# Weight sums of a seven-product matmul made in DRAM by accumulating DMAs, with DVE work of three places moved

## The reference, cut to what matters

```
layer 0: x += fox_mixer(rms_norm(x))            # 16 heads of 64, causal softmax with forget gates
         x += square(relu(h @ w_up)) @ w_down   # "ff_a", hidden width 4096
layer 1: x += mla_mixer(rms_norm(x))            # 8 heads, low-rank q and k/v, rotated parts of q and k
         x += square(relu(h @ w_up)) @ w_down   # "ff_b"
         x = rms_norm(x, final_g)
second block, conditioned on c:
         mod = silu(c) @ ada_w + ada_b          # ada_w is 1024 x 6144; six vectors of 1024
         x += g_t * norm(token_mixer(norm(x) * (1 + sc_t) + sh_t))
         x += g_c * norm(conv_ffn(norm(x) * (1 + sc_c) + sh_c))
```

## Time and profile before

| | |
|---|---|
| median of 3 runs | 1982.93 us |
| the profiled execution | 1981.71 us, span 1980.0 us |
| PE busy | 1961.3 us, 99% of the span |
| weight loads of PE | 1640.2 us, 83% |
| DVE busy | 1341.7 us, 68% |
| ACT busy | 894.3 us, 45% |
| POOL busy | 60.4 us, 3% |
| HBM traffic | 205.66 MB read, 2.13 MB written |

### The profile page before, as it was taken

One profiled execution on the slowest core, in us unless ns is written; L12 is line 12 of the kernel. 1 busy time (PEld: TensorE's weight loads), 2 busy tenths in 40 slices (PEclk: granted clock), 3 DMA queues, 4 the chain that ended last, 5 costly groups with the idle time before them and its releaser, 6 DMA issues.

```text
span 1980.0 us, 29280 instructions
## 1 busy us (share of the span) xinstructions
PE 1961.3 (99%) x10404; PEld 1640.2 (83%) x10404; DVE 1341.7 (68%) x2145; ACT 894.3 (45%) x1417; POOL 60.4 (3%) x114
## 2 busy tenths in 40 slices
PE   9999999999999999999999999999999999999999
PEld 7777789898987887898988788778888888888888
DVE  6555579687777776797787769574444686563545
ACT  4555554445444554544444443474333544432333
POOL 0000000000110110000001100000000000000000
PEclk9999999999999999999999999999999999999999
DMA  4332243323562114523226513211322412223232
GB/s 158 86 85 85 75 148 129 106 79 98 184 205 78 52 49 157 179 69 106 96 99 214 190 46 104 74 64 65 96 96 98 151 43 85 96 95 105 88 99 91
DMA packets 61292, 209.05 MB, mean 106 GB/s; under 512 B 7160, under 2 KB 10232, under 8 KB 61200
## 3 DMA queue, kind: packets, MB, share of 16 engines
q1 hardware_dynamic: 49920, 168.32, 25.8%
q0 software_dynamic: 10560, 37.28, 6.0%
q10 hardware_dynamic: 720, 2.23, 0.3%
HBM read 205.66 MB, written 2.13 MB: 105 GB/s over the span
## 4 chain that ended last, share of the span: by engine, by line
PE 94%; DVE 4%; ACT 1%; DMA 1%; issue 1%; SPq 0%; DVEq 0%; ACTq 0%
PE bank L893 23%; PE bank L895 23%; PE bank L894 23%; PE bank L1216 4%; PE bank L1218 4%; PE bank L1217 4%; PE bank L1016 1%; PE bank L1091 1%; PE bank L1075 1%; PE bank L998 1%; PE bank L1001 1%; PE bank L1043 1%; PE bank L949 1%; PE bank L951 1%; PE bank L950 1%
## 5 line engine op out<-in xcount | busy, mean ns | idle before, releaser
L893 PE MATMUL bank<-b_hi,w_hi 128*128 128x512 f32 x2060 | 813.0, 395 | 6.6 <-DVE w_lo L2764 4.0
L895 PE MATMUL bank<-b_hi,w_lo 128*128 128x512 f32 x2060 | 802.9, 390 | 0.0
L894 PE MATMUL bank<-b_lo,w_hi 128*128 128x512 f32 x2060 | 802.7, 390 | 0.0
L893 PEld LDWEIGHTS bank<-b_hi,w_hi 128*128 128x128 f32 x2060 | 387.2, 188 | 95.9 <-issue 8.2
L895 PEld LDWEIGHTS bank<-b_hi,w_lo 128*128 128x128 f32 x2060 | 387.0, 188 | 81.0
L894 PEld LDWEIGHTS bank<-b_lo,w_hi 128*128 128x128 f32 x2060 | 387.4, 188 | 80.2 <-issue 2.4
L2764 DVE TENSOR_TENSOR w_lo<-w_raw,w_hi 128x1024 fp32r<-128x1024 f32 (+3 forms) x259 | 306.8, 1185 | 210.2 <-ACT w_hi L1810 209.5
L1810 ACT ACTIVATE w_hi<-w_raw 128x1024 fp32r<-128x1024 f32 (+3 forms) x259 | 265.5, 1025 | 263.3 <-PE bank L895 253.6
L3916 DVE SCALAR_TENSOR_TENSOR arena<-bank,vec,arena 128x511 f32<-128x511 f32 x88 | 65.7, 749 | 85.8 <-ACT arena L2658 80.5
L1216 PE MATMUL bank<-parts,w_hi 128*128 128x256 f32 x384 | 108.7, 283 | 3.3 <-DVE x L3113 3.3
L1218 PE MATMUL bank<-parts,w_lo 128*128 128x256 f32 x384 | 107.9, 281 | 0.0
(11 more groups left out here) (398 smaller groups left out, 2537.9 us busy)
## 6 DMA issues: line engine op xcount, KB each, us to landing
w_raw<-in_wstream SPq DMA_DIRECT2D x253, 512.0 KB, 3.5
arena<-in_ada POOLq DMA_DIRECT2D x48, 512.0 KB, 4.3
plain<-in_wseven SPq DMA_DIRECT2D x24, 512.0 KB, 5.0
early<-in_wseven SPq DMA_DIRECT2D x24, 512.0 KB, 6.8
w_raw<-in_wstream SPq DMA_DIRECT2D x12, 384.0 KB, 3.0
arena<-crow POOLq DMA_DIRECT2D x16, 256.0 KB, 4.8
w_raw<-in_wstream SPq DMA_DIRECT2D x10, 256.0 KB, 2.6
x<-in_xT ACTq DMA_DIRECT2D x4, 512.0 KB, 6.6
```

Source lines behind the costliest of these rows:

```text
L893: nc.tensor.matmul(dst, whi, rhs_hi(k), start=(k == 0), stop=False)
L894: nc.tensor.matmul(dst, whi, rhs_lo(k), start=False, stop=False)
L895: last = nc.tensor.matmul(dst, wlo, rhs_hi(k), start=False, stop=(k == n - 1))
```

## The change

1. **Sums in DRAM.** A DRAM tensor `seven_sums` takes the sums of all 24 units. POOL makes them in *turns* (`sum_turn`): in turn t it copies two units' four blocks (group t), adds two block columns (group t - 1), one (group t - 2) and one (group t - 3), all DMAs with `accum_op=add` but the copy, each turn behind a wait for all DMAs of the turn before. Turns 0 to 9 stand in the fox attention, one behind each `rows` and then back to back; turns 10 to 14 in the mla attention. SP waits for the sums before a feed-forward's first load. `two`, `three` and `four` go; SP loads each of the seven operands by a DMA of 256 KB into a ring of eight slots.
2. **Rotated low parts** of the second attention are made by DVE (`queries_low`) ahead of the low values.
3. **Conditioning**: of mla_out's six, three stay (tiles 3 to 5), and the wait for the row of silu(c) moves from its start to tile 3; ff_b has one beside every second early up tile and every unit but the first of a chunk (18, in a third place with a single buffer), six in its last up tiles and none behind.
4. **ff_b's last down projection** is written out: each panel's split ahead of the adds, and the splits of three mixer panels one by one between them, not all three ahead.

PE's instructions and their order are the same.

```diff
+        SEVEN_RING = 8
+        GROUP = 2
+        ada_at = [..., ([plain[:, 6:8, :].rearrange("p a t -> p (a t)")] * 2, early[:, 6:8, :].rearrange("p a t -> p (a t)"))]
+        ADA_EARLY, ADA_UP, ADA_POST, ADA_FIRST = 6, 9, 6, 3
+        sum_rows = nc.dram_tensor("seven_sums", (2 * UNITS * P, 4 * T), F32, kind="Internal").ap()
@@ SP
-            def load_seven(n):
-                if n >= 2:
-                    sp.wait_ge(seven_lo, seven_count(SEVEN * (n - 1) - 1))
-                for h in range(2): ...
+            def load_seven(i):
+                if i >= SEVEN_RING and i % GROUP == 0:
+                    sp.wait_ge(seven_lo, seven_count(i - SEVEN_RING + GROUP - 1))
+                n, o = i // SEVEN, i % SEVEN
+                src, at = (seven_rows, PIECE[o]) if PIECE[o] is not None else (sum_rows, SUM_AT[o])
+                sp.dma_start(seven_raw(i), src[n * P:(n + 1) * P, at * T:(at + 1) * T]).then_inc(...)
@@ SP, ahead of the first seven loads of a feed-forward
                         sp.wait_ge(free, count)
+                        sp.wait_ge(sum_in, sum_count(SUM_GROUPS[run] + 3))
@@ POOL
+            def sum_turn(turn):
+                pool.wait_ge(sum_in, sum_count(turn))
+                for back, (to, src, at) in enumerate(((slice(0, 4 * T), seven_rows, slice(0, 4 * T)),
+                                                      (slice(0, 2 * T), seven_rows, slice(T, 3 * T)),
+                                                      (slice(2 * T, 3 * T), sum_rows, slice(0, T)),
+                                                      (slice(3 * T, 4 * T), sum_rows, slice(2 * T, 3 * T)))):
+                    if 0 <= turn - back < SUM_GROUPS["ff_b"]: ...
+                            pool.dma_start(sum_rows[units, to], src[units, at], accum_op=ALU.add).then_inc(sum_in, 16)
             rows(0, 0)
             rows(1, 1)
+            sum_turn(0)
+            for p in range(2, FOX_PAIRS):
+                pool.wait_ge(row_min, 6 * p - 6)
+                rows(p, p % 2)
+                sum_turn(p - 1)
+            for turn in range(FOX_PAIRS - 1, FOX_PAIRS + 1):
+                sum_turn(turn)
             pool.wait_ge(ctx_lo, FOX_PAIRS)
             pool.dma_start(ada_at[1][1], d["cvec"].to_broadcast([P, D])).then_inc(ada_cin, 16)
+            sum_turn(FOX_PAIRS + 1)
             pool.wait_ge(ada_silu, 1)
...
-            with pool.Fori(0, MLA_HEADS // 2) as hh:
-                for m in range(2):
-                    pool.wait_ge(rope_hi, 2 * hh + (m + 3))
-                    pool.tensor_tensor(qr_part[1][m], q_rope[m], qr_part[0][m].bitcast(F32), ALU.subtract).then_inc(rope_lo, 1)
+            for turn in range(FOX_PAIRS + 2, SUM_TURNS):
+                sum_turn(turn)
@@ DVE, mla_step
                     low_context(h - 2, 0, h + (CTX0["mla"] - 1))
+                if project:
+                    queries_low(h, m)
@@ DVE, mla_out
-                    lambda: low_context(MLA_HEADS - 1, 0, CTX0["mla"] + MLA_HEADS), lambda: dve.wait_ge(ada_cin, 48), fresh=4)
+                    lambda: low_context(MLA_HEADS - 1, 0, CTX0["mla"] + MLA_HEADS), nothing, fresh=4)
@@ DVE, end of ff_b
+                last_add(0, 0)
+                for k in range(2, KT):
+                    w_split(last + 1 + k)
+                    last_add(k - 1, (k - 1) % 2)
+                    last_post(k - 2, k % 2)
+                    if k % 2 == 0:
+                        mix_low(k // 2 - 1)
```

More of the change, by code:

```diff
@@ L683, in program, with sum_count @@
         wflat = d["wstream"]
-        def seven_src(n):
-            size = 4 * P * T
-            return d["wseven"][n * size:(n + 1) * size].rearrange("(p c) -> p c", p=P)
+        seven_rows = d["wseven"].rearrange("(r c) -> r c", c=4 * T)
+        sum_rows = nc.dram_tensor("seven_sums", (2 * UNITS * P, 4 * T), F32, kind="Internal").ap()
+        def sum_count(turn):
+            return 16 + 16 * sum(min(max(turn - back, 0), SUM_GROUPS["ff_b"]) for back in range(4))
         block = ctx.enter_context(nc.Block())
@@ L2150, in seven_ffn @@
                 j = first + n - 1
-                def last_square(j):
-                    square(j)
-                    if run == "ff_b":
-                        for p in range(MIX_W):
-                            mix_split(p)
-                segment(run, first + n, KT, last_mid, nothing, lambda: last_square(j), fresh=1)
+                if run == "ff_a":
+                    segment(run, first + n, KT, last_mid, nothing, lambda: square(j), fresh=1)
+                    return last_mid
+                square(j)
+                w_split(first + n + 1)
+                for k in range(2, KT):
+                    w_split(first + n + k)
+                    last_mid(k - 2, k % 2)
+                    if k % 2 == 0:
+                        mix_split(k // 2 - 1)
+                last_mid(KT - 2, 0)
                 return last_mid
@@ L3166, in up_tiles @@
                         else:
[L3167 to L3171 removed]
+                            low(SEVEN * QUAD * seven_chunk(run, c))
+                            low(SEVEN * QUAD * seven_chunk(run, c) + 1)
                         if not last:
@@ L3180, in up_tiles @@
                         up_conditions(run, j)
+                        if run == "ff_b":
+                            tile_condition(c, j - (first if c else 0))
                 w_split(0)
@@ L3208, in seven_ffn @@
                             w_half(c, first, i + 3 - end)
-                        if i % SEVEN == 0:
-                            four(at // SEVEN)
-                        if i % SEVEN == 2 and i + 5 < end:
-                            two(at // SEVEN + 1)
-                        if i % SEVEN == 4 and i + 3 < end:
-                            three(at // SEVEN + 1)
+                        if run == "ff_b":
+                            chunk_condition(c, i)
                         if i == 1:
@@ L3246, in lead1 @@
                         dve.sem_inc(x_sum, 2)
-                        mix_splits()
-                segment(run, last + 1, KT, last_add, last_post, lead0, lead1)
+                if run == "ff_a":
+                    segment(run, last + 1, KT, last_add, last_post, lead0, lead1)
+                    return last_add, last_post
+                w_split(last + 1)
+                lead0()
+                w_split(last + 2)
+                lead1()
+                last_add(0, 0)
+                for k in range(2, KT):
+                    w_split(last + 1 + k)
+                    last_add(k - 1, (k - 1) % 2)
+                    last_post(k - 2, k % 2)
+                    if k % 2 == 0:
+                        mix_low(k // 2 - 1)
                 return last_add, last_post
```

158 lines of the change are left out of this document (82 added, 76 removed).

## The result

The changed kernel takes 2003.4 us (median of 4 runs, 2000.53 to 2010.2) beside 1982.7 us before (4 runs, 1982.1 to 1983.48): ratio 1.0109, 95% interval 1.0083 to 1.0135. It is slower by 1.1%, where 1975.2 us had been forecast. The profiled execution is the fastest of the four: 2000.53 us, span 1998.7, 18.7 us more than before.

The account below looks back on a forecast made before the run. PE, busy 1961.3 of 1980.0 us, was taken as the bound, so only its stalls count. -3.9 - 2.1 - 3.05 + 1.4 = -7.7 gave 1974.0 us profiled, median 1975.2, own range 1973 to 1979.

Parts of the forecast that it names:

- the turn's length: POOL's DRAM sums: a full turn takes 20 us, between 15 and 28, so decay rows, panels and conditioning stay hidden.
- The prediction's 38 us: Estimated full turn if reads and writes both count against 358 GB/s; PE would lose some 85 us; chance 0.02.
- Its rival: Border from attention to ff_a: turns beyond 25.6 us make DVE wait at conditioning; 1997 us at 28; chance 0.13.
- The panels double and no more: Panel loads beside turns: a panel's own 1.3 us of transfer at 409 GB/s doubles at most; about 11 us allowed.
- TensorE's pace doesn't suffer: Whole kernel: DMA traffic alone does not slow PE's matmuls, it can only make an operand late.
- Starts of chunks: Seven-product chunks: sums leave DVE, so four PE stalls of 0.98 us go; -3.9 us.
- mla_out, -2.1: mla_out: without DVE's wait for silu(c)'s row at the start, two PE losses go; -2.1 us.
- End of ff_b: ff_b's last down projection: splits go first, mixer panels every second tile, PE's late start goes; -3.05 us.
- Rotated low parts: Second attention: DVE makes them ahead of the low values, delaying PE at even steps and the last; +1.4 us.
- Conditioning in the chunks: ff_b's chunks: single-buffer DMAs and DVE's 1.22 us each are hidden by three products' lead; 0 us.
- Loads in the chunks: Seven-product chunks: 256 KB operand loads through eight slots stay hidden; 0 us, bound above 2 us per chunk, 12.

Follow-up runs that it names:

- run without a turn after 217 us: Changed kernel with only ff_b's sums in DRAM, all nine turns in the first attention, ff_a summing on VectorE, VectorE's order changed at three places: 1977.26 us, ratio 0.9977.
- 9, 16, 23: Kernel with only ff_b's sums in DRAM, conditioning in ff_b's chunks at i = 9, 16, 23 in place of 11, 16, 21: 1973.41 us, ratio 0.9955.

## Why the prediction was wrong

**The step that failed is the turn's length, and its cost outside an attention.** The prediction took 20 us between bounds of 15 and 28, "twice for the added bytes". Measured: 27.3. The error has two parts. Twice for an added byte was right (2.1). But the 4.2 MB and 2.1 again were divided by what 87 GB/s leave of 409. The earlier trace rows has the engines 31% busy at those 87 GB/s, which is 281 GB/s for full engines, not 409. At 48.7 us of an engine per copied MB the 16 engines move 329 GB/s, and then the 19.8 us hold only with nothing beside them. With the panels' 19% it is 24.4. In the turn of 186.88 the turn's own queue took 20.6 us of all engines and the panels' 6.0, and 0.5 us stayed free; in the next one 2.7 us stayed free. The prediction's 38 us by the Trainium skill's 358 GB/s ("DMA: Bandwidth & Descriptors", Bandwidth) were not borne out either. That section gives 358 GB/s for a core when both cores of a pair stream, and 425 measured for one alone. Here the windows show 227 to 234 GB/s with the engines 93 to 95% busy.

The length was not all of it. The run with plain copies had turns of 20.1 us, the prediction's own figure, and took 1984.5 us where 1975.2 had been forecast: the silu row was in time, and late panels alone cost 3.7 and 4.4 us. Of the changed kernel's 21.7 us, 9.1 are the stall behind the silu row and 12.6 are late panels, of which 8.1 are left with the short turn.

**Its rival was the right one, by place, sign and point; that its size fitted is luck.** It said that beyond 25.6 us the silu row and `ada` are late in ff_a and the kernel is slower, 1997 us at 28. At 27.3 the row landed at 295.7 and DVE's first conditioning started at 299.88 (280.76 before). But its 22 us were all of this one stall, which cost 9.1 us; the other 12.6 are panels, which the rival did not have. It got 0.13. In hindsight, a size that no row shows, whose upper bound lies past the point of decision, deserved nearer to 0.4.

**"The panels double and no more" failed too.** It cost 8.2 us at 240 to 280 and 4.4 at 600 to 640, which no rival held. I had two rows, 3.5 and 4.2 us, and the second had one POOL transfer beside it, not four. Measured: 9.8 us in the median beside full turns, 11.4 beside plain ones, 5.3 with one transfer under way. The Trainium skill's rule that each DMA engine serves its queues in rotation, packet by packet ("DMA: Bandwidth & Descriptors", Queues, rings and completion order), was read as a doubling of the panel's own 1.3 us. The trace disagrees with that reading: 6.3 us more than the 3.5 are far over it. Nor does the price of an added byte explain it. As many added bytes as the panel has would take 0.52 x 102 / 16 = 3.3 us, an estimate of 6.9 us to land; beside plain copies it would be 5.2, where 11.4 were measured. What the packets in between cost each, no run here measured one by one, and none separates the queue's order from what DRAM itself gives.

**The same traffic costs nothing where panels are wanted seldom.** The forecast's claim that TensorE's pace doesn't suffer held: 189.15 busy of 190 us at a DMA share of 0.95. In the first attention a panel is wanted every 8.1 us (16 in 130 us) and by estimate may take about 16 with two buffers; the median of 9.8 and a longest of 16.5 hid. In fox_out, ff_a's tiles and the low stage it is every 5.4 us, so about 11 us, and landings of 6.5 to 14.1 are too near. The run without a turn after 217 us shows it from the other side: full engines up to there, no loss.

**Starts of chunks, -3.9:** right. The four stalls gave back 0.97 to 0.98 us each, 3.9; 0.4 us more per chunk follow in the next products, which the forecast did not have: -5.5 in all. **mla_out, -2.1:** right, -2.4; DVE makes its adds there without a DMA wait:

```profile
788.46 1.37 DVE L2876 TENSOR_TENSOR x<-bank,x 128x512 f32<-128x512 f32 x2 [2.84 <-PE bank L979]
```

**End of ff_b, -3.05:** right mechanism, -4.8. The stall before (2.88 us idle) had been followed by 3.4 us at half clock, a further 1.7 us, which the prediction didn't count because it looked at starts of two matmuls and not at the granted clock behind them. That stall is gone. A short wait ahead of it, on the last hidden tile's low part, is new and makes the +0.5 at 1080 to 1100:

```profile
1118.80 0.50 PE L921 MATMUL bank<-b_hi,w_hi 128*128 128x512 f32 x1 [0.16 <-DVE b_lo L3159]
```

**Rotated low parts, +1.4:** the later steps cost 1.6, much as worked out: 0.23 to 0.33 us at three even steps and 0.50 at the last. Missed was the first step, where nothing runs ahead and the logits wait at once for the queries: 2.0 us. Nine us later TensorE waited 1.7 us more, for a panel that had landed late beside a turn; 3.9 in all with small parts.

```profile
668.98 0.69 DVE L3385 TENSOR_TENSOR b_lo<-arena,b_hi 128x512 fp32r<-128x512 f32 x1
669.70 0.69 DVE L3381 TENSOR_TENSOR b_lo<-bank,b_hi 128x512 fp32r<-128x512 f32 x1
...
669.92 0.47 PE L1026 MATMUL bank<-b_hi 128*128 128x512 f32 x1 [1.99 <-DVE b_lo L3385]
```

The queries' waits, in the first step and the later ones, were a matter of order alone: without turns, moving two calls gave them all back. The panel's was the turns'.

**Conditioning in the chunks, 0:** wrong by a little, +0.65 at each of three ends. The 1.22 us at product 25 stand before the low part of the panel behind the chunk. At product 23 two ends lose nothing and one 0.3 us. **Loads in the chunks, 0:** right; no wait for them in the changed kernel.

**Sum:** the terms apart from the turns came to -5.6 us of median without turns where -7.7 was forecast; the turns added 22 us by trace and 26 in the medians.

Open: what makes a panel land late beside several transfers from DRAM to DRAM even with engines to spare; why the clock falls to half at about 1350 us of the time before in some traces (changed, without turns with either order, plain copies, 9, 16, 23) and not in others, with no stall before it that differs (1.6 us); and why the changed kernel's four runs spread over 10 us where those without turns spread over 3.5.

## What to carry to other kernels

Work that is moved to idle DMA engines must fit by engine time, with what else runs there on top, but that isn't enough: it must not stand ahead of a small transfer in one queue, and the loads beside it must have room to land late, which plain copies at 81% showed. So look at the busy share and at the landing time within each stretch, never at the span's median. If a cost that the trace doesn't show has a bound on the far side of a decision point, do half the work (here ff_b's alone, with DVE's order mended too): it was 5.7 us faster than before, and about 8 us with the conditioning moved. And after any edit that touches a software pipeline look at its first step, where no slack has been built up.

## What the runs showed of the hardware

- A DMA that adds in DRAM took an engine 2.1 times as long per byte as a copy: 102 and 49 us of one engine per MB, from the shares of POOL's queue with adds and with plain copies. One alone: 1 MB in 13.2 us, 0.5 MB in 7.4 us, where copying 2.1 MB takes 8.9 us.
- A panel of 512 KB on the sync engine's queue lands in 3.6 us in the quiet first attention, in 5.3 beside one such transfer and in 9.7 beside up to four. Beside up to four plain copies it was 11.4, though the engines were less busy (81% against 95%).
- A 4 KB transfer on the same queue as a turn, issued 7 us behind it, landed 20.4 us later; with no turn in front, 1.6 us.
- At some stalls TensorE's granted clock went to half, the 1.2 GHz level, for 3.4 or 6.8 us: at idle times of 2.88 us (before), 2.40 and 6.85 (changed), 2.08 (without turns). At 2.73, 3.38 and 1.99 us in the changed kernel it did not. Where it does, 3.4 us at half with TensorE at work cost 1.7 us more than the stall itself.
